# Router on the raw residual, two expert tiles loaded during the mixer, and earlier weight splits in two MLPs

## What is computed

```python
def _rmsnorm(x, g):
    y = x * rsqrt(mean(x * x, -1) + EPS); return y * g
def _conv_ffn(h, w_up, conv_w, conv_b, w_down):
    u = causal_depthwise_conv(h @ w_up, conv_w) + conv_b      # width 3
    gate, val = split(u, 2); return (silu(gate) * val) @ w_down
x = x + gate1 * (mix @ w_out)
hn2 = rms_norm(x, g_norm2) * (1.0 + scale2) + shift2
g_prob = softmax(hn2 @ w_router_group + b_rg)                 # 4 groups, top 1
e_logits = hn2 @ w_router_expert + b_re                       # 8 experts a group, top 2
ffn = sum of silu(h @ w_gate[e]) * (h @ w_up[e]) @ w_down[e], weighted   # 32 experts
x = x + gate2 * ffn; return rms_norm(x, g_final)
```

## Time and profile before

| | |
|---|---|
| median of 3 runs | 1418.77 us (1417.67 to 1423.01) |
| profiled execution | 1419.14 us |
| its span, first to last instruction | 1417.5 us |
| TensorE busy | 1353.1 us (95%) |
| TensorE weight load | 981.7 us (69%) |
| VectorE, ScalarE busy | 738.1 us (52%), 562.7 us (40%) |
| mean DMA rate | 263 GB/s |

### The profile page before, as it was taken

The page is one execution under the profiler, slowest core; times in us unless marked ns, Lnnn a source line. Parts: engine busy times, 40 slices in busy tenths (PEclk is TensorE's granted clock), DMA queues, the critical chain, the costliest instruction groups (busy, mean ns, idle before and its releaser), DMA issues.

```text
span 1417.5 us, 19885 instructions
## 1 busy us (share of the span) xinstructions
PE 1353.1 (95%) x7990; PEld 981.7 (69%) x7990; DVE 738.1 (52%) x1291; ACT 562.7 (40%) x856; POOL 33.3 (2%) x54
## 2 busy tenths in 40 slices
PE   7999899999999998999999998989999999999996
PEld 6988588888777997899987776755444444444442
DVE  5745546877746444688865765762222223222222
ACT  5334535555555565566654545521111111111111
POOL 1000000111000000000000000000000000000000
PEclk9999999999999999999999999999999999999998
DMA  9556343999943641255745433189999999999994
GB/s 318 206 204 241 122 145 129 323 310 320 341 166 132 212 146 60 76 192 187 248 166 178 134 119 119 60 342 419 426 427 427 429 428 428 429 429 428 429 428 192
DMA packets 112291, 372.73 MB, mean 263 GB/s; under 512 B 4300, under 2 KB 63980, under 8 KB 99552
## 3 DMA queue, kind: packets, MB, share of 16 engines
q1 hardware_dynamic: 104352, 344.07, 62.9%
q0 software_dynamic: 7872, 27.76, 5.7%
HBM read 370.75 MB, written 1.05 MB: 262 GB/s over the span
## 4 chain that ended last, share of the span: by engine, by line
PE 81%; DVE 7%; DMA 6%; ACT 4%; issue 2%; SPq 0%; ACTq 0%; DVEq 0%
PE ps L611 14%; PE ps L1429 13%; PE ps L573 8%; PE ps L574 8%; PE ps L575 8%; PE ps L1450 7%; DMA arena<-in_w_expert_up_dram 5%; PE ps L1412 4%; PE ps L588 3%; PE ps L589 3%; PE ps L590 3%; DVE w_low L510 2%; PE ps L1017 2%; PE ps L1456 1%; ACT w_high L502 1%
## 5 line engine op out<-in xcount | busy, mean ns | idle before, releaser
L510 DVE TENSOR_TENSOR w_low<-ring,w_high 128x1024 fp32r<-128x1024 f32 x264 | 311.4, 1221 | 175.6 <-ACT w_high L502 175.5
L502 ACT ACTIVATE w_high<-ring 128x1024 fp32r<-128x1024 f32 x264 | 264.8, 1052 | 214.3 <-PE ps L611 92.4
L573 PE MATMUL ps<-h_high,w_high 128*128 128x256 f32 x1088 | 314.4, 289 | 5.4 <-DVE w_low L510 4.1
L574 PE MATMUL ps<-h_low,w_high 128*128 128x256 f32 x1088 | 309.5, 285 | 0.0
L575 PE MATMUL ps<-h_high,w_low 128*128 128x256 f32 x1088 | 309.5, 284 | 0.0
L573 PEld LDWEIGHTS ps<-h_high,w_high 128*128 128x128 f32 x1088 | 210.6, 194 | 25.3 <-DVE arena L1980 12.6
L574 PEld LDWEIGHTS ps<-h_low,w_high 128*128 128x128 f32 x1088 | 210.6, 194 | 0.0
L575 PEld LDWEIGHTS ps<-h_high,w_low 128*128 128x128 f32 x1088 | 210.4, 193 | 0.0
L1429 PE MATMUL ps<-ring,arena 128*64 128x512 f32 x592 | 176.6, 594 | 5.2 <-issue 1.5
L1429 PEld LDWEIGHTS ps<-ring,arena 128*64 128x64 f32 x592 | 55.3, 137 | 116.1 <-issue 111.1
L611 PE MATMUL ps<-w_high,h_high 128*128 128x512 f32 x304 | 95.0, 394 | 4.7 <-DVE h_low L526 3.0
(11 more groups left out here) (353 smaller groups left out, 1609.2 us busy)
## 6 DMA issues: line engine op xcount, KB each, us to landing
ring<-in_ffn_w_up_dram SPq DMA_DIRECT2D x44, 1024.0 KB, 7.8
ring<-in_w_expert_gate_dram SPq DMA_DIRECT2D x19, 2048.0 KB, 27.7
ring<-in_w_expert_down_dram SPq DMA_DIRECT2D x18, 2048.0 KB, 26.1
ring<-in_w_expert_up_dram SPq DMA_DIRECT2D x18, 2048.0 KB, 24.6
ring<-in_ret_w_in_dram SPq DMA_DIRECT2D x11, 2048.0 KB, 7.9
arena<-in_w_expert_up_dram SPq DMA_DIRECT2D x11, 2048.0 KB, 26.4
ring<-in_ffn_w_down_dram SPq DMA_DIRECT2D x10, 2048.0 KB, 8.4
arena<-in_w_expert_gate_dram SPq DMA_DIRECT2D x10, 2048.0 KB, 24.1
```

The lines of the kernel that those rows point to most:

```text
L502: nc.scalar.activation(hi, raw, ACT.Copy).then_inc(hi_done, 1)
L510: last = eng.tensor_tensor(lo, raw, hi.bitcast(F32), ALU.subtract)
L573: nc.tensor.matmul(o, hi, hTh[:, k, :], start=(k == 0), stop=False)
L574: nc.tensor.matmul(o, hi, hTl[:, k, :], start=False, stop=False)
```

## The change

1. **Start.** SyncE issues tile 0 of `x` ahead of the first half of the retention weights. TensorE does six idle products of 128 columns first and nine more between the transposes of the two tiles.
2. **MLPs.** ScalarE splits half 3 right behind half 2, and VectorE does `scaled(0)`, `scaled(1)` and the low part of half 3 before the taps of pair 0. ScalarE's loop is written out.
3. **Mixer buffers.** They are packed below word 8796: some lie over others, over `hT` and over `xn`.
4. **Tiles ahead.** Homes are used in the order (8, 7, 2, 0, 1, 6, 3, 4, 5, 9). Tile 0 is issued behind the load of the fourth mixer unit, tile 1 behind that of the sixth, both after the last up half of the second MLP.
5. **Router.** Its weights are loaded at the end of the second MLP's up halves. `shift @ w_router` is summed once (one product of 288 elements and a reduction on VectorE at the end of that MLP, one TensorE product, one addition), and `scale * w_router` once at the end of `mix_out`. TensorE transposes the raw residual, with a stride of eight words, and multiplies; the root is applied to the logits. The square of tile 1 comes after ScalarE's evictions.
6. **Selection.** Fewer chained waits on VectorE; the first selection matrix is built before the expert weights; three idle products ahead of the first gather. Home 9 waits for `t_lg` 3, which is the same product as `t_lg` 2 before.

```diff
+        def late_pe(pe, r, turns=0):
             for t in range(NT):
+                if t:
+                    idle_turns(turns, 4, P)
...
+        def routed_pe(pe):
+            for t in range(NT):
+                pe.wait_ge(norm_src[ROUTED][0][0], update(4) + 2 * t)
+                turned = x[:, t, :].rearrange("p (f k) -> p k f", k=KD)
+                for j in range(4):
+                    for k in (2 * j, 2 * j + 1):
+                        last = nc.tensor.transpose(ps[:, j, (k % 2) * T + t * P:(k % 2) * T + (t + 1) * P],
+                                                   turned[:, k, :], ident)
+                    if t == NT - 1:
+                        last.then_inc(norm_tr, 1)
+                if t == 0:
+                    idle_turns(3, 4, T)
+        def routed_evict(eng, which):
+            for j in (which, which + 2):
+                eng.wait_ge(norm_tr, 4 * N_TR[ROUTED] + j + 1)
+                dst = hT[:, 2 * j:2 * j + 2, :].rearrange("p a b -> p (a b)")
+                if which == 0:
+                    nc.scalar.activation(dst, ps[:, j, :], ACT.Copy).then_inc(norm_ha, 1)
+                else:
+                    nc.vector.tensor_copy(dst, ps[:, j, :]).then_inc(norm_hv, 1)
...
-        HOMES = (2, 6, 7, 8, 0, 1, 3, 4, 5, 9)
+        HOMES = (8, 7, 2, 0, 1, 6, 3, 4, 5, 9)
...
+            sp.dma_start(x[:, 0, :], x_tiles[:, 0, :]).then_inc(x_in[0], 16)
             first = rows(A["ret_w_in"][0])
             sp.dma_start(wide[0][:, :, 0:T], first[:, :, 0:T]).then_inc(first_in, 16)
-            sp.dma_start(x[:, 0, :], x_tiles[:, 0, :]).then_inc(x_in[0], 16)
...
+            AHEAD = [phases["mix_in"][3], phases["mix_in"][5]]
+                if n in AHEAD:
+                    sp.wait_ge(up_h, 2 * FP)
+                    dst, src, done = expert_tile(AHEAD.index(n))
+                    sp.dma_start(dst[:, :, :], src).then_inc(done, 16)
...
-            pool.wait_ge(b_oc, 4)
+            pool.wait_ge(up_h, 2 * FP)
             pool.dma_start(wr[:, :, 0:NG], ...)      # and three more, as before
...
             pe.wait_ge(ident_in, 16)
-            late_pe(pe, 0)
+            idle_turns(6, 4, P)
+            late_pe(pe, 0, 9)
...
             norm_pe(pe, 5, 10)
+            nc.tensor.matmul(ps[:, 7, 0:NR], ones, shift_sum, start=True, stop=True).then_inc(t_lg, 1)
...
-            norm_pe(pe, 6, 7)
-            normed_whole(pe, 6)
-            pe.wait_ge(r_in, 64)
+            routed_pe(pe)
             for t in range(NT):
                 for k in range(KD):
+                    if t == 0 and k % 2 == 0:
+                        pe.wait_ge(norm_hv if k // 2 % 2 else norm_ha, 2 + k // 4 + 1)
...
             nc.tensor.matmul(ps[:, 5, 128:128 + NE], ones, asg[:, 1, :], start=False, stop=True).then_inc(t_lg, 1)
+            idle_turns(3, 6, T)
...
+                def pair(n):                          # ScalarE, 22 times, no loop
+                    if n == 0:
+                        next_high(2)
+                        next_high(3)
+                    elif n > 1:
+                        next_high(n + 2)
...
+            for t in range(NT):                       # ScalarE, router
+                act.wait_ge(norm_src[ROUTED][0][0], update(4) + 2 * t)
+                if t:
+                    routed_evict(act, 0)
+                nc.scalar.activation(xn[:, t, :], x[:, t, :], ACT.Square, accum_out=stat[:, t:t + 1]).then_inc(norm_ss, 1)
+            late_sqrt(act, 6)
...
-                    if n:                             # VectorE, MLP pair n
-                        scaled()
-                    if n + 2 < FP:
+                    if n > 1:
+                        scaled(n)
+                    if n == 1:
+                        pass
+                    elif n + 2 < FP:
                         split_low(dve, f"up{l}", n + 2)
                     if n == 0:
                         late_rows(dve, link, r)
-                        scaled()
+                        scaled(0)
+                        scaled(1)
+                        split_low(dve, f"up{l}", 3)
...
                 split_low(dve, ("sb_v", "mix_in")[l], 0)
+                if l:
+                    dve.wait_ge(r_in, 64)
+                    link(nc.vector.tensor_tensor(shifted, wr, mods[:, 3, :].unsqueeze(2).broadcast_to([P, KD, NR]), ALU.mult))
+                    nc.vector.tensor_reduce(shift_sum, shifted.rearrange("p k n -> p n k"), AX, ALU.add)
                 residual(dve, f"down{l}")
...
+            nc.vector.tensor_tensor(wrs, wr, mods[:, 2, :].unsqueeze(2).broadcast_to([P, KD, NR]), ALU.mult)
...
+            routed_evict(dve, 1)
             norm_dve(dve, link, 6)
-            norm_evict(dve, 6, 1)
...
+            for t in range(NT):
+                last = nc.vector.scalar_tensor_tensor(out=lg[:, t, :], in0=lgp[:, t, :], scalar=stat[:, 6 + t:7 + t], in1=br,
+                                                      op0=ALU.mult, op1=ALU.add)
+            link(last)
...
+            select(sel, 0, None, False, m_s)          # behind the ranks, ahead of the expert weights
```

More of the change, by code:

```diff
@@ L850, in last_downs @@
                     sp.dma_start(dst[:, 2:4, :], src[:, 2:4, :]).then_inc(done, 16)
-            for N in range(NS):
+            for N in range(len(AHEAD), NS):
                 home = HOMES[N]
@@ L1613, in pair @@
                     last.then_inc(up_id, 1)
-                    act.wait_ge(up_cv, off + (FP * l + 2 * b + j + 1))
-                    nc.scalar.activation(cv[:, j, 0:T], cv[:, j, 0:T], ACT.Silu).then_inc(up_si, 1)
-                    if l == 0 and j == 1 and (split is not None or b < 2):
-                        ada_evict(off, b)
+                    act.wait_ge(up_cv, FP * l + n + 1)
+                    nc.scalar.activation(cv[:, n % 2, 0:T], cv[:, n % 2, 0:T], ACT.Silu).then_inc(up_si, 1)
@@ L1619, in ffn @@
+                    if l == 0 and n % 2 and n + 1 < FP:
+                        ada_evict(n // 2)
                 if l == 0:
                     nc.scalar.activation(credit[:, 5:6], small[:, 0:1], ACT.Copy).then_inc(ada_ev, 2)
-                with act.Fori(0, 2) as i:
-                    nc.scalar.activation(credit[:, 7:8], small[:, 0:1], ACT.Silu)
-                    for b in range(4):
-                        for j in range(2):
-                            pair(b, j, i * 8, i)
-                for b in range(3):
-                    for j in range(2):
-                        pair(b, j, 16, None)
+                nc.scalar.activation(credit[:, 7:8], small[:, 0:1], ACT.Silu)
@@ L1630, in ada_rest @@
+                for n in range(FP):
+                    pair(n)
                 def ada_rest(h):
```

173 lines of the change are left out of this document (92 added, 81 removed).

## The result

The changed kernel took 1412.95 us (median of 7 runs, 1409.21 to 1415.36), the kernel before 1419.22 (7 runs, 1417.67 to 1423.01): a ratio of 0.995, 95% interval 0.9933 to 0.9966. Forecast were 1403.7 us and a range of 1399.5 to 1410.5. The kernel is faster, but by 6.3 us and not by 15. The profiled execution took 1409.59 (span 1407.9), 9.6 us less than that of before.

The account below looks back on a forecast made before the run. Expert-weight transfers were taken to set the end, with TensorE only 4.4 us ahead. Start -0.4, MLPs +4.2, end of `down1` -0.1 and experts +11.4 sum to 15.1; 1418.8 - 15.1 = 1403.7 us, range 1399.5 to 1410.5.

Parts of the forecast that it names:

- Start: Kernel start: first product about 1.4 us later, at most 1.6 us back from slow passes; -0.4 us, ends +0.5 and -1.4.
- Clock: TensorE's granted clock: 1.55 us more in the second MLP without its fall, 1.7 us saved in the gathers.
- MLPs: Both MLPs: waits of 1.13 and 2.17 us go, 0.6 comes back, 1.55 of clock is gained; sum 4.2 us.
- End of `down1` and mixer: VectorE's extra product and reduction ahead of the residual cost 0.1 us (0 to 0.5); mixer additions cost 0, at most 0.4.
- Router: Residual to first gate product: logits 5.7 us earlier, first gather 7.7, gathers save 1.7; first gate product 9.4 earlier.
- Experts: Expert tile stream: rests, starts anew at tile 10 and still sets the end; tile 93 lands 11.4 us earlier.
- Tiles ahead: Two expert tiles loaded in the mixer: cost 0, ends 0 and 1; without them most of the router's gain is lost.
- A: Gathers: idle products and denser work hold the full clock, gathers take 3.8 us; 1402.4 us; 15%.
- B: Router: raw transposes cost up to four times, clock stays down, half 4 late; gain 9, 1409.7 us; 17%.
- C: Expert stream: some early tiles late, stream never rests, moves 9.8 us instead of 11.4; 1405.3 us; 10%.
- D: ScalarE's straight code: fetching it stops ScalarE, kernel slower than before, 1434 us at 1.3 us a pair; 2%.
- E: Whole change: each gain given back, the MLPs wait for half 4 and the ranks come late; 1414 us; 4%.

Follow-up runs that it names:

- old start: Changed kernel with the earlier kernel's start: first weights issued ahead of x tile 0, no idle products there; 1406.01 us (7 runs), again 1405.73 us (6 runs).
- the variants: Four kernels, each the changed kernel with the start edits taken back and one further edit; 1408.9 us in the mean (24 runs).
- the second profile: Profile of the changed kernel run again with no edit; 1413.07 us (7 runs), ratio 0.9949.
- the restart in halves: Changed kernel with the old start, expert tiles 10 and 11 issued in halves, the first halves during the first gate product; 1405.19 us (6 runs).
- both edits: Changed kernel with the old start, the restart in halves, and two of four products ident by x moved behind the first gather; 1412.16 us (6 runs).

## Why the prediction was wrong

The mechanisms were mostly right; three sizes were not, and the largest miss is the start. The forecast has 15.1 us, of which the start is -0.4 and the clock 3.25 (1.55 in the second MLP, 1.7 in the gathers). Measured: the means of the runs differ by 8.6, the medians by 7.1 over all runs and 6.3 over the first seven.

The kernel with the old start tells where the 6.5 us between 15.1 and 8.6 went. Without its start term the forecast is 15.5. Measured without the start edits, 14.2 (mean 1421.0 to 1406.8): 11.0 of work (even time 1421.3 to 1410.3, where 12.25 was said) and 3.3 of clock (4.8 us less lost, by 0.68). So 1.3 of the miss lie in the other terms and 5.3 in the start: -0.4 was said, -5.7 measured. How much of that is the start's own is less sure, since the variants with the old start lost more to the clock. Against their mean it is -3.6, and then the clock's 3.25 is overbooked by some 3.

- *Start, the step that failed most.* "I take -0.4, nearly the middle", with a delay of 1.4 us and ends of +0.5 and -1.4. The delay of the first split is 2.0, beyond the worse end by itself, and it is 3.0 at half 3 of the first projection (1.5 in the second profile). What the forecast feared in half a sentence, "then the slow stretch may come all the same", is what happened: TensorE rests 4.0 us, 27, 16 and 17 passes are slow where 17 were, and nothing comes back. The full cost is 5.7 us in the means (3.6 against the variants), some 2 to 3 of it work. The rest is clock lost later, which the term put at nothing; its cause is open.
- *Clock, the second.* "Behind the 2.17 us rest the granted clock was at 0.50 ... that is 1.55 us more", and likewise 1.7 in the gathers. Both places came out as said or better (1.00 at 602, the gather in 3.84 us). But a fall seen at one place of one profile was booked as time that goes away. The MLP edit alone left the lost time where it was (17.6 and 18.1), and the whole change has 20.1, which is 16.7 to 18.4 if its start is counted as in before: no gain. With the old start it is 12.8, the gain as forecast, and 17.1 in the variants, hardly any. The record does not settle which holds.
- *MLPs.* 2.65 without the clock; 1.4 and 2.9 measured. The waits were read rightly: 1.2 and 3.0 us in the profiled pair (the 3.0 with the fall that is gone), and half 4 late by 0.7 where 0.6 was said.
- *End of `down1` and mixer.* 0.1; 0.5 in the profiled pair.
- *Router.* Logits 5.7 us earlier: 5.7 (946.43 - 933.61 = 12.8 against 7.1). From there to the assignment 5.06: 4.99. First gather 7.7 earlier: 7.1 (15.7 us after the last residual's start, against 22.9). The 0.6 between is explained by the four products ident by x, which ran mostly at the lower clock, to 947.2, and stood ahead of the ranks; the forecast forgot that queue. With the gather at 3.84 the first gate product comes 9.5 earlier where 9.4 was said, or 10.1 against the residual. The transposes with a stride took 1.16 us for eight where the earlier trace rows has 1.97 for sixteen, starts 0.12 to 0.13 us apart in both. The Trainium skill's "SBUF — State Buffer", section "Door 1: The DMA port swizzle", says that each access which crosses to a new line of 16 bytes pays a penalty; the forecast's estimate from it was twice the time. This trace does not show a penalty for TensorE's reads.
- *Experts.* The stream was said to come 11.4 earlier and came 9.6. "The stream ran without a gap" in the kernel before isn't quite right: its windows show the rate falling just when tile 10 is issued, at 972.04:
```profile
971.00:972.00 1.00, 1.00 (x6) 0.20 (x2) 0.00 (x0) 0.11 (x1) 0.00 (x0) 1.00 1.07 459
972.00:973.00 1.00, 1.00 (x6) 0.34 (x6) 0.74 (x2) 0.49 (x1) 0.00 (x0) 1.00 0.54 229
973.00:974.00 1.00, 1.00 (x8) 0.37 (x6) 0.01 (x1) 0.00 (x0) 0.00 (x0) 1.00 1.30 344
974.00:975.00 1.00, 1.00 (x8) 0.35 (x6) 0.00 (x0) 0.00 (x0) 0.00 (x0) 1.00 0.83 328
```
Against 430 GB/s these three windows lack some 0.9 us of transfers (an estimate), so the queue was nearly empty. Still tile 10 landed at 980.9 (8.9 us after its issue), 4.9 behind home 9 as the forecast counts. What it had too short is the other side. Its sum of 0.2 + 2 + 84 x 4.90 lets tile 10 land 7.1 us after the first gate product; it landed 7.95 after it (962.41 to 970.36), and the 83 tiles behind it took 407.7 us for 406.7. That is 1.8 us. From tile 10's issue to tile 93's landing it was 415.65 us before and 415.5 after a real rest of 6 us: the stream moves by what the first gate product moves by.
- *Tiles ahead.* "That is all they do" holds, and their price is now measured: 11.1 us. The rest before tile 10 was forecast (8 us; the transfers stand still for 6, from some 957 to 963), and TensorE's waits for expert tiles, forecast at 2.4, are 4.0, since both moved together.
- *Rivals.* A (full clock in the gathers) was right in its place and worthless in its sum. B, C, D did not come: transposes and ScalarE's straight code cost nothing that a row shows. E's time, 1414, was nearest, but its reasons (the MLPs wait for half 4, the ranks come late) gave back little, 0.7 and 0.6 us; its nearness is luck.

The best version found is the changed kernel with the old start: 1406.0 us over 13 runs, against 1413.0 and 1420.1, and with the restart in halves 1405.2 over 6, which the runs do not tell from it in the median.

## What to carry to other kernels

Price the clock over many runs, with the mean granted clock beside each time, and not by the falls of one profile: a fall that was gone at one place was not shown to be gone from the sum. Look at the pace of the passes too where the clock column reads 1.00 from the start. A small edit at the start deserves a run of its own before it is bundled with others: here it took back some third of the gain. Idle products ahead of a gap bought nothing. A stream of loads into few homes moves with the work that frees them, so earlier first tiles pay only as long as the homes keep up.

## What was not expected of the hardware

The granted clock mostly falls in pieces of 1.7 us lost or twice that (5.1 and 6.8 in the profile of both edits, at 542 and 942), at some of the same places in kernels that differ much (543 to 547, 864 to 867), and one kernel's runs lose between 8 and 21 us (the old start), or 13 and 25 (the changed kernel). Each us lost so costs 0.68 us of time, not 1. After a standstill the transfers are back at their full rate of 430 GB/s within 3 to 4 us of the issue (49 GB/s from 960 to 964, 348 from 964 to 968, 430 behind it, with the issue at 962.56).
